# Up projections of a gated MLP in float32 parts: 18 of 22 tile pairs per layer in seven half-width products (Strassen's scheme) in place of eight

## The reference, cut to what matters

```python
def conv_ffn(h, w_up, conv_w, conv_b, w_down):
    u = h @ w_up                               # (512, 1024) @ (1024, 5632)
    gate, val = jnp.split(u, 2, axis=-1)
    gp = jnp.pad(gate, ((0, 0), (CONV_W - 1, 0), (0, 0)))
    gate_c = conv_b + sum(conv_w[j] * gp[:, j:j + S] for j in range(CONV_W))
    return (jax.nn.silu(gate_c) * val) @ w_down
```

## Time and profile before

| | |
|---|---|
| Three runs | 1092.51, 1092.82, 1094.67 us; median 1092.82 us |
| Profiled execution, first to last instruction | 1091.2 us |
| TensorE busy, share of the span | 1082.8 us, 99% |
| VectorE, ScalarE, GpSimd busy | 539.4, 428.5, 50.3 us |
| Mean granted TensorE clock | 0.999 of full speed |
| Up stage of layer 0 (226.8 to 455.6 us) | 228.8 us, TensorE busy throughout |

### The profile page before, as it was taken

How to read it: one execution, slowest core, us unless ns; L and a number is a source line. 1 busy time by engine, 2 the same in 40 slices (tenths; PEclk the granted TensorE clock), 3 DMA queues, 4 the chain that set the end, 5 groups by cost and what they waited for, 6 DMA issues and landing times.

```text
span 1091.2 us, 14756 instructions
## 1 busy us (share of the span) xinstructions
PE 1082.8 (99%) x5526; PEld 907.6 (83%) x5526; DVE 539.4 (49%) x809; ACT 428.5 (39%) x747; POOL 50.3 (5%) x51
## 2 busy tenths in 40 slices
PE   9999999999999999999999999999999999999998
PEld 8888888798888888888889987789888888888886
DVE  7544578654443434333366587664343434523344
ACT  6511456543232323222355377753323232422242
POOL 1100211000000000000000024200000000000000
PEclk9999999999999999999999999999999999999999
DMA  9332327333423232122272542122333333313231
GB/s 286 108 106 81 113 86 228 73 107 88 115 77 114 78 115 77 38 97 96 96 193 58 152 100 78 20 78 87 106 87 106 89 103 93 99 35 98 95 137 77
DMA packets 154821, 111.10 MB, mean 102 GB/s; under 512 B 35536, under 2 KB 140144, under 8 KB 154784
## 3 DMA queue, kind: packets, MB, share of 16 engines
q1 hardware_dynamic: 153776, 107.41, 33.4%
q0 software_dynamic: 864, 2.92, 0.9%
q10 hardware_dynamic: 144, 0.26, 0.1%
HBM read 106.87 MB, written 2.13 MB: 100 GB/s over the span
## 4 chain that ended last, share of the span: by engine, by line
PE 96%; DVE 2%; SPq 1%; ACT 0%; issue 0%; DMA 0%; DVEq 0%
PE ps L1555 18%; PE ps L1556 18%; PE ps L1557 18%; PE ps L1802 7%; PE ps L1803 7%; PE ps L1804 7%; PE ps L1747 2%; PE ps L1749 2%; PE ps L1748 2%; PE ps L1636 1%; PE ps L1638 1%; PE ps L1637 1%; PE ps L1897 1%; PE ps L1928 1%; PE ps L1910 1%; SPq L429 1%
## 5 line engine op out<-in xcount | busy, mean ns | idle before, releaser
L1555 PE MATMUL ps<-act_hi,w_hi 128*128 128x512 f32 (+1 forms) x1016 | 368.8, 363 | 1.8 <-DVE act_lo L1015 1.7
L1556 PE MATMUL ps<-act_lo,w_hi 128*128 128x512 f32 (+1 forms) x1016 | 366.4, 361 | 0.0
L1557 PE MATMUL ps<-act_hi,w_lo 128*128 128x512 f32 (+1 forms) x1016 | 366.4, 361 | 0.0
L1555 PEld LDWEIGHTS ps<-act_hi,w_hi 128*128 128x128 f32 x1016 | 191.7, 189 | 33.3 <-DVE act_lo L1015 2.1
L1556 PEld LDWEIGHTS ps<-act_lo,w_hi 128*128 128x128 f32 x1016 | 191.8, 189 | 29.0 <-issue 0.2
L1557 PEld LDWEIGHTS ps<-act_hi,w_lo 128*128 128x128 f32 x1016 | 191.7, 189 | 29.1
L1802 PE MATMUL ps<-w_hi 128*128 128x512 f32 x288 | 112.0, 389 | 0.0
L1803 PE MATMUL ps<-w_lo,w_hi 128*128 128x512 f32 x288 | 112.0, 389 | 0.0
L1804 PE MATMUL ps<-w_hi,w_lo 128*128 128x512 f32 x288 | 112.0, 389 | 0.0
L789 ACT ACTIVATE arena<-ps,vecs 128x512 f32<-128x512 f32 x44 | 34.3, 780 | 188.6 <-PE ps L1557 188.6
L1317 DVE SCALAR_TENSOR_TENSOR arena<-ps,vecs,arena 128x511 f32<-128x511 f32 x44 | 33.0, 750 | 144.4 <-ACT arena L789 144.4
(11 more groups left out here) (212 smaller groups left out, 1217.0 us busy)
## 6 DMA issues: line engine op xcount, KB each, us to landing
raw<-in_f_w_up SPq DMA_DIRECT2D x88, 512.0 KB, 4.6
raw<-in_f_w_down SPq DMA_DIRECT2D x44, 512.0 KB, 3.4
raw<-in_m_w_in SPq DMA_DIRECT2D x23, 512.0 KB, 4.3
raw<-in_m_w_out SPq DMA_DIRECT2D x8, 512.0 KB, 3.4
raw<-in_a_w_in SPq DMA_DIRECT2D x16, 256.0 KB, 4.7
raw<-in_a_w_out SPq DMA_DIRECT2D x16, 256.0 KB, 4.8
h<-in_x SPq DMA_DIRECT2D x4, 512.0 KB, 7.7
h<-in_x_turned SPq DMA_DIRECT2D x3, 512.0 KB, 7.0
```

Source lines behind the costliest of these rows:

```text
L1555: nc.tensor.matmul(dst, uh[:, k], zh, start=(k == 0), stop=False)
L1556: nc.tensor.matmul(dst, uh[:, k], zl, start=False, stop=False)
L1557: ins = nc.tensor.matmul(dst, ul[:, k], zh, start=False, stop=(k == KT - 1))
```

## The change

Pairs 0 to 3 of each layer stay as they were (`PLAIN = 4`). For pairs 4 to 21 the product of a pair is cut in two along K, along the tokens, and into gate and value. These are eight products of 4 slices of K x 128 channels x 256 tokens; Strassen's scheme makes seven of them, `product` in the code, each of 12 matmuls of 256 columns.

For this it needs sums of blocks on both sides. On the token side four sums are made once per layer (`first_sums`, `last_sums`, 8 VectorE operations of 128x1024) and split into hi and lo (`form_hi`, 4 on ScalarE; `form_lo`, 4 on VectorE). On the weight side there are seven forms of 128x512 per pair: three are blocks of the raw tiles, four are sums. VectorE makes two sums (`near_sums`), then GpSimd two that build on the first of them and on each other (`weight_sums`). ScalarE rounds all seven in four casts (`raw_hi` twice, `sum_hi` twice), VectorE makes the low parts in four subtractions (`raw_lo` twice, `sum_lo` twice). The sums lie where the low parts are written, so the first `sum_lo` waits until both of GpSimd's sums are there.

On the result side one half bank is accumulated over the first, third, fifth and seventh product, and ScalarE copies it out in between (`part`, four copies of 128x256 a pair), so TensorE's third, fourth, fifth and seventh product each wait for a copy. VectorE joins the parts in three additions of 128x256 (`gate_first`, `gate_last`, `val_first`).

The diff, cut to its core (buffers, semaphores and the unchanged inner statements of the loops left out):

```diff
+    PLAIN = 4
+    SEVENS = FT - PLAIN
+    HT = S // 2
...
     SLOT = [0, 1, 2, 3, 7] + [n % 4 for n in range(QK_UNITS - FIRST + V_UNITS + O_UNITS)]
-    FFN_SLOTS = [4 + n % 4 for n in range(2 * FT)] + [n % 2 for n in range(FT - TAIL)]
+    FFN_SLOTS = [4 + n % 4 for n in range(2 * PLAIN)]
...
+        sums = nc.alloc_sbuf_tensor_at("sums", [P, 2, 8, D // 2], F32, offset=w_lo_at)
...
+            def weight_sums(l, m, t):
+                n = l * SEVENS + t - PLAIN
+                val = raw[:, 2 * t + 1]
+                lo = sums[:, t]
+                first, last = slice(0, QW), slice(QW, 2 * QW)
+                pool.wait_ge(raw_in[2 * t + 1], m * 16 + landed(G_UP[l] + 2 * t + 1))
+                pool.wait_ge(near_sum, m * 4 + 2 * n + 1)
+                nc.gpsimd.tensor_tensor(lo[:, 4], lo[:, 5], val[:, first], ALU.subtract).then_inc(s_sum, 1)
+                pool.wait_ge(s_sum, m * 4 + 2 * n + 1)
+                nc.gpsimd.tensor_tensor(lo[:, 6], val[:, last], lo[:, 4], ALU.subtract).then_inc(s_sum, 1)
+            def ffn_sums(l):
+                with pool.Fori(PLAIN // 2, FT // 2) as m:
+                    for t in range(2):
+                        weight_sums(l, m, t)
+            ffn_sums(0)
             s = SLOT[G_AIN + 2]
...
+                def sum_hi(m, t, j):
+                    n = l * SEVENS + t - PLAIN
+                    act.wait_ge(s_sum, m * 4 + 2 * n + 1 + j)
+                    act.wait_ge(near_sum, m * 4 + 2 * n + 2 - j)
+                    fs = slice(3 + 2 * j, 5 + 2 * j)
+                    ins = nc.scalar.copy(forms_hi[t][:, fs], sums[:, t, fs])
+                    if j == 0:
+                        ins.then_inc(f_hi, 1)
+                    else:
+                        ins.then_inc(w_hi_done, 2)
...
+                def part(m, t, r):
+                    n = l * SEVENS + t - PLAIN
+                    act.wait_ge(product_mm, m * 12 + 6 * n + (1, 2, 3, 5)[r])
+                    src = ps[:, 2 * t, 0:HT] if r == 1 else ps[:, 2 * t + 1, HT:]
+                    dst = first_part[:, t] if r == 0 else parts[:, r - 1]
+                    nc.scalar.copy(dst, src).then_inc(part_done, 1)
...
+                def seven(m, t, nm, nt):
+                    part(m, t, 0)
+                    if nt is None:
+                        split_hi(down)
+                    else:
+                        raw_hi(nm, nt, False)
+                    part(m, t, 1)
+                    if nt is not None:
+                        raw_hi(nm, nt, True)
+                    part(m, t, 2)
+                    if nt is None:
+                        split_hi(down + 1)
+                    else:
+                        sum_hi(nm, nt, 0)
+                        sum_hi(nm, nt, 1)
+                    part(m, t, 3)
+                    if nt is None:
+                        for j in range(2):
+                            nc.scalar.copy(hid_pair[j][0], hid[:, j]).then_inc(hid_hi, 1)
+                    joined_conv(m, t)
...
+                def conv(i, t, join=None):
...
                     dve.wait_ge(silu_done, i * 2 + n)
                     dve.wait_ge(w_used, i * 4 + counted(up + 2 * t + 1))
...
+                    if l == 0:
...
+                    link(nc.vector.tensor_tensor(t1, t4, h0a, ALU.subtract))
+                    nc.vector.tensor_tensor(t1, t1, l0a, ALU.subtract).then_inc(t_sum, 1)
+                    dve.wait_ge(t_sum, 4 * l + 1)
...
+                    nc.vector.tensor_tensor(t2, t3, t1, ALU.subtract).then_inc(t_sum, 1)
+                    dve.wait_ge(t_sum, 4 * l + 2)
+                    nc.vector.tensor_tensor(t3, t3, t4, ALU.subtract).then_inc(t_sum, 1)
+                    dve.wait_ge(t_sum, 4 * l + 3)
+                    link(nc.vector.tensor_tensor(t4, h1a, t2, ALU.subtract))
+                    nc.vector.tensor_tensor(t4, t4, l1a, ALU.add).then_inc(t_sum, 1)
...
+                    gate, val, lo = raw[:, 2 * t], raw[:, 2 * t + 1], sums[:, t]
+                    dve.wait_ge(raw_in[2 * t], m * 16 + landed(up + 2 * t))
+                    dve.wait_ge(w_used, m * 4 + counted(up + 2 * t - 3))
+                    nc.vector.tensor_tensor(lo[:, 5], gate[:, 0:QW], gate[:, QW:], ALU.add).then_inc(near_sum, 1)
+                    dve.wait_ge(raw_in[2 * t + 1], m * 16 + landed(up + 2 * t + 1))
+                    nc.vector.tensor_tensor(lo[:, 3], val[:, 0:QW], gate[:, 0:QW], ALU.subtract).then_inc(near_sum, 1)
...
+                    n = l * SEVENS + t - PLAIN
+                    if j == 0:
+                        dve.wait_ge(f_hi, m * 6 + 3 * n + 3)
+                        dve.wait_ge(s_sum, m * 4 + 2 * n + 2)
+                    else:
+                        dve.wait_ge(w_hi_done, m * 4 + up + 2 * t + 2)
+                    fs = slice(3 + 2 * j, 5 + 2 * j)
...
+                def gate_first(m, t):
+                    n = l * SEVENS + t - PLAIN
+                    dve.wait_ge(product_mm, m * 12 + 6 * n + 4)
+                    dve.wait_ge(part_done, m * 8 + 4 * n + 3)
+                    nc.vector.tensor_tensor(ps[:, 2 * t, 0:HT], ps[:, 2 * t, 0:HT], parts[:, 1], ALU.add)\
+                        .then_inc(joined, 1)
...
+                def seven(m, t, nm, nt):
+                    if nt is None:
+                        split_lo(down)
+                    else:
+                        near_sums(nm, nt)
+                        raw_lo(nm, nt, False)
+                        raw_lo(nm, nt, True)
+                    gate_first(m, t)
+                    if nt is None:
+                        split_lo(down + 1)
+                    else:
+                        sum_lo(nm, nt, 0)
+                    gate_last(m, t)
+                    if nt is None:
+                        for j in range(2):
+                            lo_hid(j)
+                    else:
+                        sum_lo(nm, nt, 1)
+                    conv(m, t, lambda: val_first(m, t))
+                first_sums()
+                conv(0, 0)
...
+                with dve.Fori(PLAIN // 2, FT // 2 - 1) as m:
+                    seven(m, 0, m, 1)
+                    seven(m, 1, m + 1, 0)
+                seven(FT // 2 - 1, 0, FT // 2 - 1, 1)
+                seven(FT // 2 - 1, 1, None, None)
...
-                with pe.Fori(1, FT // 2) as i:
+                for n in range(2, PLAIN):
+                    t = n % 2
+                    pe.wait_ge(hid_done, l * FT + n + 1)
+                    for q in range(2):
+                        pe.wait_ge(w_lo_done, counted(up + 2 * n + q))
+                        project(4 + 2 * t + q, 2 * t + q).then_inc(w_used, 1)
...
+                def product(t, form, z, bank, ts, start):
+                    dst = ps[:, bank, ts]
+                    for k in range(KT // 2):
+                        cs = slice(k * P, (k + 1) * P)
+                        uh, ul = forms_hi[t][:, form, cs], forms_lo[t][:, form, cs]
+                        zh, zl = z[k]
+                        nc.tensor.matmul(dst, uh, zh, start=(start and k == 0), stop=False, skip_group_check=not start)
+                        nc.tensor.matmul(dst, uh, zl, start=False, stop=False, skip_group_check=not start)
+                        ins = nc.tensor.matmul(dst, ul, zh, start=False, stop=(k == KT // 2 - 1),
+                                               skip_group_check=not start)
+                    return ins
...
+                pe.wait_ge(t_form_lo, 4 * (l + 1))
+                with pe.Fori(PLAIN // 2, FT // 2) as m:
                     for t in range(2):
-                        pe.wait_ge(hid_done, i * 2 + (l * FT + t + 1))
-                        pe.wait_ge(w_lo_done, i * 4 + counted(up + 2 * t))
-                        project(4 + 2 * t, 2 * t).then_inc(w_used, 1)
-                        pe.wait_ge(w_lo_done, i * 4 + counted(up + 2 * t + 1))
-                        project(5 + 2 * t, 2 * t + 1).then_inc(w_used, 1)
+                        n = l * SEVENS + t - PLAIN
+                        first, last = slice(0, HT), slice(HT, S)
+                        gate, val, other = 2 * t, 2 * t + 1, 6 + t
+                        pe.wait_ge(hid_done, m * 2 + (l * FT + t + 1))
+                        pe.wait_ge(f_lo, m * 6 + 3 * n + 1)
+                        product(t, 0, z1a, val, last, True).then_inc(product_mm, 1)
+                        pe.wait_ge(f_lo, m * 6 + 3 * n + 3)
+                        product(t, 3, t3, gate, first, True).then_inc(product_mm, 1)
+                        pe.wait_ge(part_done, m * 8 + 4 * n + 1)
+                        product(t, 4, t2, val, last, False).then_inc(product_mm, 1)
+                        pe.wait_ge(part_done, m * 8 + 4 * n + 2)
+                        product(t, 2, t4, gate, first, False).then_inc(product_mm, 1)
+                        pe.wait_ge(part_done, m * 8 + 4 * n + 3)
+                        pe.wait_ge(w_lo_done, m * 4 + counted(up + 2 * t + 1))
+                        product(t, 5, t1, val, last, False).then_inc(product_mm, 1)
```

(83 more changed lines are left out.)

105 lines of the change are left out of this document (94 added, 11 removed).

## The result

The changed kernel takes 1107.1 us (1107.00, 1107.06 and 1107.20), the kernel before, run beside it, 1092.7 us (median of 1092.51, 1092.64, 1092.82 and 1094.67): a ratio of 1.0129, 95% interval 1.0113 to 1.0145. A fourth execution of the changed kernel took 2024.67 us at a granted clock of 0.532, for a reason that no trace shows, and is left out of every comparison. The change makes the kernel slower, as forecast, but by 14.4 us and not by 37.4. The profiled execution spans 1105.3 us.

A forecast was written before the change was run, and what follows sets the result against it. TensorE, busy 99%, was taken as the bound. Per layer, 18 x -0.80 = -14.4, first pair +5.6 and 16 pairs x 1.72 = +27.5 make +18.7; two layers +37.4 on 1092.8 give 1130.2 us, range 1092 to 1148.

The forecast's parts named there:

- 10.88 to 10.08 us a pair: TensorE's matmuls in a seven-product pair: 0.80 us less per pair, -28.8 us in all if nobody makes TensorE wait.
- VectorE for itself: VectorE's own work per seven-product pair, without holds by GpSimd: 8.99 us, which fits in TensorE's 10.08.
- GpSimd and VectorE exclude each other: Operations of VectorE with two SBUF inputs and operations of GpSimd exclude each other for their length.
- the first rival: GpSimd goes in turn, between VectorE's operations: VectorE loses about 1.14 us twice, round 11.27, time 1110 us; chance 0.25.
- So VectorE's operations that follow without a gap keep GpSimd out: GpSimd's first sum waits until `raw_lo` is through, then VectorE waits: round 11.8 us, 16 pairs x 1.72 = +27.5 per layer.
- The first seven-product pair: VectorE's and ScalarE's queues are late at each layer's first such pair: second product 1.6, third 2.3, seventh 1.7, together +5.6 us.
- The last pair free: Each layer's last seven-product pair makes no forms for another and waits for nothing.
- the start of the down stage: The reordered start (blocks 2, 0, 3, 1 of 1.36 us each) covers the last multiplication.
- The lower ends of two times: With GpSimd's sums at 1.04 us, not 1.27: first rival about 1093 us, forecast 1112.
- The page's rule: Shared ports are an exclusive lock, issue order decides who blocks: GpSimd would precede `raw_lo`, giving the first rival's time.
- the forecast's own mechanism: VectorE's operations without a gap keep GpSimd waiting until `raw_lo` is through: round 11.8 us, time 1130.2 us; chance 0.50.

## Why the prediction was wrong, point by point

- **TensorE: right.** 10.88 to 10.08 us a pair was the term; TensorE left to itself takes 10.00. The price of a half-width matmul in the earlier trace rows holds.
- **VectorE for itself: right.** 8.99 us added up. The measured rounds less what was moved or held give 11.29 - 1.10 - 1.09 = 9.1 and 10.29 - 1.22 = 9.1.
- **That GpSimd and VectorE exclude each other: right**, for two-input operations, 1.09 to 1.10 us each time; the prediction had 1.14 for it in the first rival.
- **"So VectorE's operations that follow without a gap keep GpSimd out": wrong, and the step that failed.** It was taken from one operation of another form than the new ones. The forecast therefore let GpSimd wait until `raw_lo` was through and VectorE stand idle for both of GpSimd's sums and for the cast and copy behind them: L610 recorded at 3 us or more, an idle VectorE ahead of its first `sum_lo`, 1.7 us of TensorE before the seventh product, a round of 11.8. Measured were 1.67 us, no idle time of VectorE there, 0.87 us and 11.29. With GpSimd's sums served in turn, VectorE's round is 11.27 by the prediction's own working. Over 32 pairs the difference of 0.5 is 16 us of the 23 missed.
- **The first seven-product pair: too dear.** 5.6 us in the forecast, 4.2 in the rival; against 10.00 it lost 2.4 us in layer 0 and 2.1 in layer 1. The second product waited for nothing (1.6 us in the forecast), the third 1.6 and 1.2 us (2.3), the seventh 0.7 (1.7). With the cheaper matmuls this is 3.4 us per layer, the other 7 of the 23.
- **The last pair free: nearly right** (10.13 us against 10.00). Nothing for loads, clock and the start of the down stage: right; the granted clock is 1.00 in the profiled execution.
- **The time.** What was measured between the starts of the pairs accounts for it: 18 x -0.88 + 2.3 + 0.1 + 16 x 1.29 = +7.2 per layer, +14.4 in all.
- **The lower ends of two times.** With GpSimd at 1.04 us the prediction has about 1093 us for the first rival and 1112 for the forecast. Its own working takes 2 x 0.23 us from each of 32 rounds and at most as much from the two first pairs, and gives about 1095 and 1115. The measured hold didn't need that end.
- **The page's rule.** The Trainium skill, SBUF — State Buffer, section "Who interferes with whom", has issue order decide who blocks; by the prediction that was 1110 us. The trace agrees for two-input operations (1107.1, GpSimd asks at 332.90 and goes before L1526). It doesn't for a `tensor_scalar` with a column on GpSimd: that asked before the second low part started and yet let it pass in all 40 pairs, and got in only behind the third of four.

The range began at 1092 and held the time, and the sign was right; but 1107 lies below the 1112 to 1148 us that the forecast's own mechanism reaches, so the range owes the hit to the rival in it. The likelier of two mechanisms was picked by a row that resembled the case less than it seemed.

## What to carry to other kernels

Work given to GpSimd isn't free for VectorE: a two-input float32 operation of 128x512 took 1.10 us of VectorE's time where VectorE would have made it in 0.61. It cost VectorE nothing only where it fell beside work of VectorE that reads PSUM. Place matters more than the count: with the same sums on the same engines the change cost 14 us, and gained 29 us with VectorE's two sums ahead of the last join. And before a row is used for who waits for whom, its instructions must be of the same form as the new ones.

## What the runs showed of the hardware that was not expected

- A `tensor_scalar` of GpSimd with a scalar column waits longer for VectorE's two-input operations than other forms do: 2.50 us on average for 128x256, while two low parts passed at 1.218 each. It isn't kept out for good: behind the third of four low parts it got in and held the fourth for 0.20 us (128x256) or 0.41 (128x512). A `tensor_scalar` with numbers, a copy and a two-input subtraction, each of 128x512, get in behind the operation that runs (holds of 0.41, 0.41 and 1.09 us).
- 84 matmuls of 256 columns, each with a weight load of its own, took 10.00 us, 0.119 each, where TensorE didn't wait. In the changed kernel the granted clock of layer 0's up stage was 1.00, though TensorE stood for 0.87 us in every pair.
